# Output products of two token tiles and six rows begun at the end of the gated recurrence, the last head's result kept on chip, and the recurrence's score levels in compact form

## The reference

```
def step(S, blk):                     # one chunk
    qc, vc, kc, gc = blk
    b = cumsum(gc)
    o = (qc * exp(b)) @ S             # part that comes from the state
    A[t, s] = sum_d qc[t,d] * exp(b[t,d] - b[s,d]) * kc[s,d]   for s <= t
    o = o + A @ vc                    # part from inside the chunk
    S = exp(b_end) * S + (kc * exp(b_end - b)).T @ vc
    return S, o
...
g_y = heads_rmsnorm(o_forward + o_backward, g_norm_g, 4) * silu(gz)
y_y = hyena_branch(...) * silu(yz)
y = concatenate([g_y, y_y]) @ w_out   # 1024 x 1024
x = x + gate * y;  result = rmsnorm(x, final_norm_g)
```

## Time and profile before

| | us |
|---|---|
| median of 3 runs | 2481.95 (2480.49 to 2482.28) |
| the profiled execution's own time | 2474.39 |
| its span | 2472.6 |
| TensorE busy in the span | 2309.8 (93%) |
| VectorE / ScalarE / GpSimd busy | 1404.3 / 799.5 / 250.3 |
| mean granted clock of TensorE | 0.972 |

### The profile page before, as it was taken

One profiled execution on the slowest core, in us unless ns is written; L12 is line 12 of the kernel. 1 busy time (PEld: TensorE's weight loads), 2 busy tenths in 40 slices (PEclk: granted clock), 3 DMA queues, 4 the chain that ended last, 5 costly groups with the idle time before them and its releaser, 6 DMA issues. The chain is left out here.

```text
span 2472.6 us, 51425 instructions
## 1 busy us (share of the span) xinstructions
PE 2309.8 (93%) x22460; PEld 1428.5 (58%) x22460; DVE 1404.3 (57%) x2260; ACT 799.5 (32%) x1493; POOL 250.3 (10%) x282
## 2 busy tenths in 40 slices
PE   6999999999999988998988998999998999998698
PEld 4444456666544448888874443444785775756343
DVE  3320345553358667887884444654694878788414
ACT  4121213224355644443332221101102445454301
POOL 0000000000012221112221113331100000000100
PEclk8999999999989999999999998999999999999899
DMA  8100122121056654433316322110231100000313
GB/s 330 60 19 7 45 76 75 62 78 63 16 153 167 176 151 109 108 94 94 95 43 222 128 86 67 51 45 32 93 121 58 36 27 27 20 17 11 145 62 116
DMA packets 132173, 209.19 MB, mean 85 GB/s; under 512 B 15677, under 2 KB 95165, under 8 KB 128366
## 3 DMA queue, kind: packets, MB, share of 16 engines
q1 hardware_dynamic: 118542, 156.07, 20.2%
q0 software_dynamic: 13408, 49.84, 7.0%
HBM read 155.34 MB, written 50.53 MB: 83 GB/s over the span
## 5 line engine op out<-in xcount | busy, mean ns | idle before, releaser
L737 PE MATMUL psum<-arena,shared 128*128 128x512 f32 (+1 forms) x864 | 328.7, 525 | 1.5 <-PEq L223 1.5
L2842 PE MATMUL psum<-arena,second_shared 128*128 128x512 f32 (+1 forms) x640 | 281.7, 566 | 11.0 <-PEq L3616 6.4
L737 PEld LDWEIGHTS psum<-arena,shared 128*128 128x128 f32 x864 | 157.0, 191 | 108.8 <-issue 101.8
L2842 PEld LDWEIGHTS psum<-arena,second_shared 128*128 128x128 f32 x640 | 111.9, 194 | 76.0 <-issue 70.7
L1243 PE MATMUL psum<-shared,arena 128*128 128x512 f32 x320 | 149.8, 617 | 0.0
L2244 PE MATMUL psum<-shared,fin_mix 128*128 128x512 f32 x320 | 143.4, 601 | 3.0 <-POOL fin_mix L2377 3.0
L1901 ACT COPY r_half<-psum 128x512 f32<-128x512 f32 x100 | 58.7, 587 | 151.8 <-PE psum L1831 151.7
L3095 DVE COPY_PREDICATED g_pairs<-g_masks,psum 128x512 f32<-128x512 uint8 x128 | 93.3, 729 | 21.0 <-PE psum L2871 21.0
L2244 PEld LDWEIGHTS psum<-shared,fin_mix 128*128 128x128 f32 x320 | 59.8, 192 | 75.0 <-issue 71.5
L1243 PEld LDWEIGHTS psum<-shared,arena 128*128 128x128 f32 x320 | 60.2, 196 | 73.4 <-issue 72.9
L2052 DVE COPY_PREDICATED r_inv<-shared,psum 128x512 f32<-128x512 uint32 x100 | 73.4, 734 | 39.9 <-PE psum L1840 39.2
(11 more groups left out here) (451 smaller groups left out, 4258.8 us busy)
## 6 DMA issues: line engine op xcount, KB each, us to landing
arena<-scratch_operands SPq DMA_DIRECT2D x152, 128.0 KB, 2.7
shared<-in_l_w_in SPq DMA_DIRECT2D x22, 512.0 KB, 3.7
scratch_spill<-shared POOLq DMA_DIRECT2D x16, 640.0 KB, 3.3
second_shared<-in_l_w_in SPq DMA_DIRECT2D x20, 512.0 KB, 3.8
scratch_operands<-arena POOLq DMA_DIRECT2D x14, 640.0 KB, 8.2
scratch_operands<-arena POOLq DMA_DIRECT2D x28, 320.0 KB, 11.3
shared<-in_l_mod_w SPq DMA_DIRECT2D x8, 1024.0 KB, 9.2
t_matrix<-in_transform SPq DMA_DIRECT2D x8, 1024.0 KB, 4.8
```

Source lines behind the costliest of these rows:

```text
L737: last = nc.tensor.matmul(p.psum[:, FILL + f % BANKS, 0:width], weight[:, q % PIECES, k, :], hT[:, k, at:at + width], start=(k == 0), stop ...
L2842: last = nc.tensor.matmul(bank[:, 0:width], w[:, kk, :], hT[:, kk, first:first + width], start=(kk == 0), stop=(kk == KT - 1))
```

## The change

It does four things. (1) A level's products of all 8 chunks go to one PSUM bank, side by side, in columns of the block's own width; levels 0 to 4 and the diagonal (`small_level`) are merged by one masked copy of 128x256 each into a new tile `near`; levels 5 and 6 are copied by ScalarE straight to their place in `pairs` (`copy_wide`, three copies per unit), and after a head's second direction `expand` copies `near` into the diagonal blocks of `pairs` (four copies per head). (2) `pairs` and `near` are kept per head instead of per unit: the diagonal is done once per head with the sum of both directions' keys (`both_keys`), and the product `pairs` x v is made in the backward unit alone. (3) After the scan, TensorE begins the output products: rows 4 and 5 of the mix for tiles 0 and 1, then the turns of head 3, then rows 6, 7, 0 and 1 for the same tiles; `stage_output` leaves these out. (4) The last head's gated result is written straight to its place in the arena instead of to DRAM; the mix's row 2 is loaded in `stage_hgrn`, and `stage_output` loads no row.

```diff
-OUT_AHEAD = (4, 5, 6, 7, 0, 1)
-OUT_ROWS = (*OUT_AHEAD, 2, 3)
+OUT_AHEAD = (4, 5, 6, 7, 0, 1, 2)
+OUT_ROWS = (*OUT_AHEAD, 3)
+OUT_BEGUN_ROWS, OUT_BEGUN_TILES = 6, 2
...
-                for k in OUT_ROWS[len(OUT_AHEAD):]:
-                    sp.dma_start(mixT[:, k, at:TOK], mix[k, :, at:TOK]).then_inc(rows_loaded[k], 16)
...
-                    pe.wait_ge(rows_loaded[k], 32)
-                    for i in range(4):
+                    pe.wait_ge(rows_loaded[k], 32 if k in OUT_AHEAD else 16)
+                    for i in range(OUT_BEGUN_TILES if row < OUT_BEGUN_ROWS else 0, 4):
...
                         pool.wait_ge(sig["fill_copied"], first_of["turn", head] + part + 1)
-                        nc.gpsimd.tensor_tensor(mixT[:, columns], mixT[:, columns], z[:, head % 2, columns], ALU.mult).then_inc(sig["gated"], 1)
+                        last_head = head == H - 1
+                        to = arena[:, head * TOK + CTX:(head + 1) * TOK] if last_head else mixT
+                        nc.gpsimd.tensor_tensor(to[:, columns], mixT[:, columns], z[:, head % 2, columns], ALU.mult).then_inc(sig["gated"], 1)
+                        if last_head:
+                            continue
...
-                pool.wait_ge(sig["stored"], 32 * H)
+                pool.wait_ge(sig["stored"], 32 * (H - 1))
...
-                    for c in range(4 * g, 4 * g + 4):
+                    for c in range(G_LAT_CHUNKS):
                         for key, query, size in blocks(n, d):
-                            at = (c - 4 * g) * C + query
-                            last = nc.tensor.matmul(p.psum[key:key + size, SCORES + m % RING, at:at + size],
+                            last = nc.tensor.matmul(p.psum[key:key + size, SCORES + m % RING, c * size:(c + 1) * size],
...
-                    scan, levels = u >= 0, w < U and 1 <= i <= L + 1
+                    scan, levels = u >= 0, w < U and 1 <= i <= levels_of(w)
...
+                        if d == 1 and i == CTX_TILES:
+                            pe.wait_ge(sig["evicted"], WIDE_COPIES * (u + 1))
+                            pe.wait_ge(sig["expanded"], C // SMALL * (h + 1))
                         pe.wait_ge(sig["state_ready"], (SLOTS - 1) * u + i)
-                        nc.tensor.matmul(out_bank, pairs[:, u % 2, lat, :], v[:, h % 2, c, :], start=True, stop=False)
+                        if d == 1:
+                            nc.tensor.matmul(out_bank, pairs[:, h % 2, lat, :], v[:, h % 2, c, :], start=True, stop=False)
...
+                def begin_output(row):
+                    k = OUT_ROWS[row]
+                    pe.wait_ge(p.out_rows_loaded[k], 32)
+                    for i in range(OUT_BEGUN_TILES):
+                        lhsT = mixT_next[:, k, (CTX_TILES + i) * P:(CTX_TILES + i + 1) * P]
+                        for n in range(2):
+                            nc.tensor.matmul(p.psum[:, 2 * i + n, :], lhsT, out_weight[:, k, n * BANK:(n + 1) * BANK],
+                                             start=(row == 0), stop=False)
...
+                for row in range(2):
+                    begin_output(row)
                 fill_to(due[LAST])
+                for row in range(2, OUT_BEGUN_ROWS):
+                    begin_output(row)
...
+                def copy_wide(w, n):
...
+                    act.wait_ge(sig["scores_ready"], m + 1)
...
+                    for key, query, size in blocks(n, d):
+                        src = p.psum[key:key + size, SCORES + m % RING, 0:G_LAT_CHUNKS * size].rearrange("p (c t) -> p c t", t=size)
+                        nc.scalar.copy(pairs[key:key + size, h % 2, :, query:query + size], src).then_inc(sig["evicted"], 1)
+
+                def expand(h):
+                    act.wait_ge(sig["merged"], (2 * SMALLS + 1) * (h + 1))
+                    for at in range(0, C, SMALL):
+                        nc.scalar.copy(pairs[at:at + SMALL, h % 2, :, at:at + SMALL], near[at:at + SMALL, :, :]).then_inc(sig["expanded"], 1)
...
                         take_exps(w, i)
+                        if i - 1 in range(SMALLS, L):
+                            copy_wide(w, i - 1)
+                        if i == L + 2 and units[w][1] == 1:
+                            expand(units[w][0])
...
+                    if d == 1:
...
+                        nc.vector.tensor_tensor(both_keys[:, :], k[:, 0, CTX:TOK], k[:, 1, CTX:TOK], ALU.add).then_inc(sig["both_keys"], 1)
...
-                    nc.vector.copy_predicated(pairs[:, w % 2, 4 * g:4 * g + 4, :], mask(units[w][1], n),
-                                              chunked(p.psum[:, SCORES + m % RING, :])).then_inc(sig["merged"], 1)
+                    src = p.psum[:, SCORES + m % RING, 0:G_LAT_CHUNKS * SMALL].rearrange("p (c t) -> p c t", t=SMALL)
+                    nc.vector.copy_predicated(near[:, :, :], mask(d, n), src).then_inc(sig["merged"], 1)
...
-                    if w < U and 1 <= i <= L + 1:
-                        merge(w, i - 1, 0)
                     if w < U:
                         scale(w, i)
-                    if w < U and 1 <= i <= L + 1:
-                        merge(w, i - 1, 1)
+                    if w < U and 1 <= i <= levels_of(w) and small_level(i - 1):
+                        merge(w, i - 1)
```

More of the change, by code:

```diff
@@ L2655 @@
 G_LAT_CHUNKS = LAT // G_CHUNK
+G_SMALL, G_SMALL_LEVELS = 32, 5
 def const_hgrn():
-    s, t = np.arange(P)[:, None], np.arange(P)[None]
+    s, t = np.arange(P)[:, None] % G_SMALL, np.arange(G_SMALL)[None]
     out = []
@@ L2664, in const_hgrn @@
         before = (s < t) if d == 0 else (s > t)
-        for n in range(G_LEVELS):
+        for n in range(G_SMALL_LEVELS):
             out.append(before & ((s >> (n + 1)) == (t >> (n + 1))) & ((s >> n) != (t >> n)))
@@ L2684, in stage_hgrn @@
              "scaled", "scores_ready", "merged", "keys_turned", "keys_copied", "update_ready", "state_ready", "outputs_ready",
-             "y_copied", "silu_ready", "squares_ready", "means_ready", "roots_ready", "normed", "gated", "stored")
+             "y_copied", "silu_ready", "squares_ready", "means_ready", "roots_ready", "normed", "gated", "stored", "both_keys", "evicted", "expanded")
     sig = {n: p.semaphore("g_" + n) for n in names}
@@ L2742, in stage_hgrn @@
     keys_bank, update_bank, out_bank = p.psum[:, KEYS, 0:P], p.psum[:, OUT, P:2 * P], p.psum[:, OUT, 0:P]
-    group = lambda w, n, g: 2 * (L + 1) * w + 2 * n + g
+    levels_of = lambda w: L + units[w][1]
+    groups_before = lambda w: (2 * L + 1) * (w // 2) + L * (w % 2)
+    group = lambda w, n: groups_before(w) + n
+    SMALL, SMALLS = G_SMALL, G_SMALL_LEVELS
+    WIDE_COPIES = 3
+    small_level = lambda n: n < SMALLS or n == L
+    merges_to = lambda w, n: (2 * SMALLS + 1) * (w // 2) + SMALLS * (w % 2) + min(n, SMALLS) + 1 - (SMALLS < n < L)
+    copies_to = lambda w, n: WIDE_COPIES * w + (2 if n == SMALLS else 3)
+    of_group = [(w, n) for w in range(U) for n in range(levels_of(w))]
     def blocks(n, d):
-        size = max(32, 1 << n) if n < L else 32
-        if n == L or 2 << n <= size:
-            return [(at, at, size) for at in range(0, C, size)]
+        if small_level(n):
+            return [(at, at, SMALL) for at in range(0, C, SMALL)]
+        size = 1 << n
         return [(at + d * size, at + (1 - d) * size, size) for at in range(0, C, 2 * size)]
@@ L2766, in stage_hgrn @@
         k = sb("k", [P, 2, TOK])
+        both_keys = sb("both_keys", [P, LAT])
         pairs = sb("pairs", [P, 2, G_LAT_CHUNKS, C])
+        near = sb("near", [P, G_LAT_CHUNKS, SMALL])
         ends = sb("ends", [P, 2, TILES])
@@ L2854, in fill_to, with scores @@
                         done[0] += 1
-                def scores(w, n, g):
+                def scores(w, n):
                     h, d = units[w]
-                    m = group(w, n, g)
-                    if g == 0 and n < L:
+                    m = group(w, n)
+                    if n < L:
                         pe.wait_ge(sig["scaled"], (L + 2) * w + n + 1)
-                    elif g == 0:
-                        pe.wait_ge(sig["k_ready"], w + 1)
+                    else:
+                        pe.wait_ge(sig["both_keys"], h + 1)
                         pe.wait_ge(sig["fill_copied"], last_of["q", h])
                     if m >= RING:
-                        pe.wait_ge(sig["merged"], m - RING + 1)
-                    left = level(w, n) if n < L else k[:, w % 2, CTX:TOK]
+                        before = of_group[m - RING]
+                        if small_level(before[1]):
+                            pe.wait_ge(sig["merged"], merges_to(*before))
+                        else:
+                            pe.wait_ge(sig["evicted"], copies_to(*before))
+                    left = level(w, n) if n < L else both_keys
                     right = level(w, n) if n < L else q[:, h % 2, :]
-                    for c in range(4 * g, 4 * g + 4):
+                    for c in range(G_LAT_CHUNKS):
```

(6 more changed lines are left out.)

44 lines of the change are left out of this document (28 added, 16 removed).

## The result

The change takes 2455.68 us in the median of 4 runs (2453.14 to 2460.47) against 2481.68 us (4 runs, 2480.49 to 2482.28): the ratio is 0.9898, 95% interval 0.9883 to 0.9913, or 26.0 us. The forecast was 28.7 us. The profiled execution took 2457.76 us with a span of 2456.0.

What follows compares the result with a forecast made beforehand. TensorE, busy 93% of the span, was taken to bound the kernel, with VectorE pacing unit 6. Terms -15.3 - 3.0 - 5.3 - 1.5 - 3.6 = -28.7 us took 2482.0 to 2453.3 us; 8-in-10 range 2444 to 2463.

Steps and rivals of the forecast that it cites:

- Part 1: Seam and output stage: 24 output products begun in the hole after the scan, plus clock kept up; -15.3 us.
- C: Seam: begun rows land later, TensorE stalls 4 to 8 us, time 2457 to 2461 us; chance 0.10.
- The clock term: Output stage start: with TensorE at work through the seam, 1.4 us of slow clock are booked back.
- Part 2: Recurrence: diagonal level gone in 4 of 8 units, -3.0 us; `pairs` x v gone in forward units, -5.3 us.
- Part 3: VectorE in the recurrence: fewer, smaller merges; -1.5 us in units 0 to 5 and -3.6 in unit 6.
- I take -1.5: Units 0 to 5: TensorE's 3.3 us of waits on scale shrink by about half, -1.5 us.
- Unit 6: VectorE-paced steps shorten to 3.97 us with a merge and 3.61 without; -3.6 us.
- Part 4: ScalarE: 24 wide copies and 16 of `expand` added, some 1.3 us per unit, 1.4 more per backward unit, hidden.
- Rival A: Only the tail arrives; ScalarE's place in the chain cancels the recurrence's gain, time 2467 us; chance 0.12.
- B: Recurrence gains more: waits in units 4 and 5 go, unit 6 falls towards 3.05 us a step; 2446 us; chance 0.15.
- D: Slower: the chain gaps, exponential, scale, merge paces every step; at 6.1 us a step, 2493 us; chance 0.03.

Runs made afterwards that it cites:

- tail alone: Kernel before with only the begun output products, the last head kept on chip and row 2 loaded ahead, old recurrence: ratio to before 0.9944.
- add twice: Changed kernel with the sum of both directions' keys made twice in its place: ratio to before 0.9913.
- wide copies twice: Changed kernel with each of ScalarE's wide copies made twice, the second over the first: ratio to before 0.9917.
- add later, merge first: Changed kernel with the both-directions key sum moved to step 5 of the backward unit and the masked copy ahead of scale: ratio to before 0.9881.

## Why the prediction was right, and where it was off

**Part 1, the begun output products: right in size and in steps.** Forecast 15.3 us, measured 15.4 in the first pair of profiles. The wait for the first row was put at 1.2 us and is 1.42; the output stage was to start 23.4 us after the scan's end and does. The experiments part it: 3 us for the head that stays on chip, 12 for the hole. The rival that rows land too late (C) is out: no begun row but the first waited. The clock term was real, and it isn't certain to be earned: the tail alone loses 1.7 us to it behind the same wait, where I had booked 1.4 as a gain.

**Part 2, products taken off TensorE: right.** The lead lost 1.0 us to the removed diagonal, a little more than the 0.75 I took (my own terms, 0.69 and 0.1, make 0.79). Units 0, 2 and 4 lost 2.1, 1.7 and 2.3 us for 1.8 forecast each, and putting such products back cost 1.8, 1.5 and 1.1. So in unit 4 half of the gain is something other than the product.

**Part 3, VectorE: this is the term that was mis-sized.** Two sentences failed. "`both_keys` adds 4 adds of 1024 elements, about 1.2 us each, where VectorE has 25% to spare": the spare share is an average, and the add was put where there is none, behind the scale of step 7 and ahead of the copy of y that TensorE waits for. Three of the four stand in waits of 3.9 us in all; moving the add gave 3.2 of them back, and doubling it added 3.8 us of waits. And "I take -1.5" for shorter waits: in units 0 to 5 the waits on scale went from 3.3 to 3.7 us. The removed diagonal, 0.8 to 1.0 us in each of units 1, 3 and 5 (read with the add moved, less the waits left), and the 3.9 us of waits nearly cancel, as the unit table shows. Unit 6 was right: 3.2 us for 3.6, and 0.438 us in the mean for the masked copy that was put at 0.45.

**Part 4, ScalarE: right for the change, not in its reserve.** The copies take 0.36 and 0.57 us out of PSUM and 0.40 for `expand`, the estimate made for it (four of them are 1.6 us per head, not the 1.4 written), and no wait of TensorE names them. But doubled they cost 3.2 us, 1.7 of them clock. They stand in the chain ahead of the copy of y in units 3 and 5, so "so it is hidden" holds in most steps and not there.

**Unit 7: outside the sum.** It grew by 1.3 us without an edit in it. TensorE stands there for the load of head 3's z weight in all kernels (4.0 us before, 4.1 after), and the clock falls to half: before for 3.4 us, from 2307.5, as the wait ends; after for 6.8 us, from 2304.0, 1.0 us before it ends. Of the fourteen profiles the seven with 3.4 us have a unit 7 of 28.9 to 29.3 us, whichever kernel it is, and the seven with 6.8 us one of 29.8 to 30.4. Why the one or the other comes stays open.

Sum of the recurrence: lead -1.0, forward units 0, 2, 4 -6.2, backward units +1.1, unit 6 -3.2, unit 7 +1.3, by the unrounded times -7.9, against -13.4. Of the 5.5 us that are missing, the waits on y are 3.9, the shorter waits that didn't come 1.5, unit 7 1.3 and unit 6 0.4; against them the removed products gave some 1.5 us more than booked.

The median's 26.0 us lies 2.7 above the 23.3 of the profiles; that is inside the interval of the ratio, 3.7 us to either side. The forecast of 28.7 is nearer to the median than to the stages it was worked out for, and that much of the agreement is luck. Rival A (the recurrence gives nothing), B (it gives more) and D (slower) are all out. A had named ScalarE's place in the chain, and a part of that is real. D's sum was off without effect: 54 steps of 0.7 us less 28.7 make 9 us, not 11.

## What to carry to other kernels

Where an engine is idle for a quarter of a stretch, ask in which steps. What a new instruction costs there depends on what stands behind it in the row; here the same add cost 3.2 us in one place and 0.7 in another. A filled hole at the seam of two stages gives back its idle time and, where the products keep the clock up, the slow start of the next stage too: here about 9.7 and 2.5 us. And cut profiles at a mark just ahead of the change: here the stages repeated within 0.3 us while what lay ahead of them scattered by 14.

## What the runs showed of the hardware

The granted clock of TensorE fell to half, its 1.2 GHz level, after waits much shorter than the 16.7 us hole. Behind a 2.75 us wait (add twice, unit 1) it was at half for 3.4 us. Behind a wait of 1.89 us it fell in one kernel (wide copies twice, unit 5) and not in another (add twice, unit 3). In unit 6 it fell in all fourteen, within 3 us of the end of a 2.0 us wait at the unit's start, which another of 1.5 to 3.1 us follows; for 6.8 us in twelve of them and for 3.4 us in two. Behind the begun rows' first wait it fell with 1.50 us of wait (tail alone) and 1.35 us (add later, merge first), and stayed up in eight profiles with waits of 1.36 to 1.64 us, 1.42 in the change. So the length of the wait doesn't decide it there. Four stretches of the kernel with both edits, where the last scan product starts at 2325.84 and the begun rows at 2327.58, against one of the changed kernel:
```profile
2326.00:2328.00 2.00, 0.65 (x4) 0.33 (x3) 0.61 (x2) 1.40 (x2) 1.70 (x2) 1.00 1.02 393
2328.00:2330.00 2.00, 2.00 (x4) 0.86 (x3) 1.66 (x4) 1.79 (x3) 0.57 (x1) 0.62 0.98 334
2330.00:2332.00 2.00, 2.00 (x4) 0.75 (x3) 0.84 (x1) 1.70 (x2) 0.00 (x0) 0.53 1.01 389
2332.00:2334.00 2.00, 2.00 (x6) 0.88 (x5) 0.00 (x0) 0.00 (x0) 0.00 (x0) 1.00 1.02 418
```
```profile
2333.00:2335.00 2.00, 2.00 (x6) 0.84 (x5) 1.66 (x4) 1.79 (x3) 0.31 (x1) 1.00 0.98 301
```
Before the fall TensorE had a scan step of small products and transposes and then the wait; it fell when the dense rows had already begun. The same begun rows behind the same wait, to 0.1 us, cost 1.7 us more or not by something that these runs don't show. A term of that size at a seam should stand in a range, not in a sum.
